# A two-layer hybrid backbone on one core: the passage between the layers and the norm behind the output projection, rearranged

## The reference, cut to what matters

```python
def rms_norm(x, g):
    return x * lax.rsqrt(jnp.mean(x * x, axis=-1, keepdims=True) + EPS) * g

def layer(x, ctx, ...):
    hx = modulate(rms_norm(x, g_pre_mix), sh1x, sc1x)       # first norm
    hc = modulate(rms_norm(ctx, g_pre_mix), sh1c, sc1c)
    px = hx @ w_in                                          # kv | q | conv b,c,u | fourier f | gates
    pc = hc @ w_in                                          # in the last layer only its kv columns
    ...                                                     # attention, short convolution, Fourier mixing
    x = x + g1x * rms_norm(yx, g_post_mix)                  # yx = (gated sum of branches) @ w_out
    hx2 = modulate(rms_norm(x, g_pre_ffn), sh2x, sc2x)      # second norm
    x = x + g2x * rms_norm(moe(hx2), g_post_ffn)            # the same for ctx in layer 0

def moe(t):
    scores = sigmoid(t @ w_router)                          # 32 experts, the best 4 of each token
    comb = weights of the four choices, scaled to sum 2.5
    routed = sum over choices of comb * expert(t)           # silu(t @ gate) * (t @ up) @ down
    return routed + shared_expert(t)
```

## Time and profile before

| what | value |
|---|---|
| median of three runs | 1566.01 us (1560.89, 1566.01, 1567.47) |
| the profiled execution: its own time | 1567.75 us |
| the profiled execution: span | 1566.0 us |
| PE busy | 1464.3 us (94%) |
| DVE busy | 947.9 us (61%) |
| ACT busy | 616.9 us (39%) |
| POOL busy | 326.2 us (21%) |
| mean granted TensorE clock | 0.979 of full |

### The profile page before, as it was taken

One profiled execution on the slowest core, in us unless ns is written; L12 is line 12 of the kernel. 1 busy time (PEld: TensorE's weight loads), 2 busy tenths in 40 slices (PEclk: granted clock), 3 DMA queues, 4 the chain that ended last, 5 costly groups with the idle time before them and its releaser, 6 DMA issues.

```text
span 1566.0 us, 22775 instructions
## 1 busy us (share of the span) xinstructions
PE 1464.3 (94%) x7739; PEld 1042.5 (67%) x7739; DVE 947.9 (61%) x1624; ACT 616.9 (39%) x1049; POOL 326.2 (21%) x392
## 2 busy tenths in 40 slices
PE   5999998899989899999999986999899899999996
PEld 2688575688867766777777744876799775555552
DVE  1777889779986466777777757446656641222222
ACT  2432235433324435656656524433555521111211
POOL 4000000001112003555556536000001021111200
PEclk9999999999999999999999997999999999999998
DMA  9943340266586155999999974516255459999993
GB/s 334 326 162 112 135 162 1 84 216 213 188 289 250 54 219 206 342 365 368 362 366 377 362 234 155 197 35 239 81 197 208 157 218 372 376 414 415 414 415 146
DMA packets 116888, 382.36 MB, mean 244 GB/s; under 512 B 13554, under 2 KB 18114, under 8 KB 98128
## 3 DMA queue, kind: packets, MB, share of 16 engines
q1 hardware_dynamic: 100976, 352.08, 59.6%
q0 software_dynamic: 14480, 26.11, 4.9%
q10 hardware_dynamic: 1360, 3.23, 0.5%
HBM read 382.05 MB, written 21.06 MB: 257 GB/s over the span
## 4 chain that ended last, share of the span: by engine, by line
PE 77%; DVE 9%; DMA 7%; ACT 2%; issue 2%; POOL 2%; SPq 0%; ACTq 0%; POOLq 0%; DVEq 0%
PE ps L1844 7%; PE ps L1814 6%; PE ps L1416 6%; PE ps L1643 4%; PE ps L1645 4%; PE ps L1644 4%; PE ps L1789 4%; PE ps L1788 4%; PE ps L1790 4%; PE ps L1847 4%; PE ps L1777 3%; DMA ring<-in_w_up_e 3%; PE ps L1539 2%; PE ps L1540 2%; PE ps L1541 2%; PE ps L1862 2%
## 5 line engine op out<-in xcount | busy, mean ns | idle before, releaser
L2464 DVE TENSOR_TENSOR ring_lo<-ring,m_lo 128x1024 fp32r<-128x1024 f32 x128 | 156.1, 1223 | 11.9 <-ACT m_lo L1285 2.4
L1285 ACT ACTIVATE m_lo<-ring 128x1024 fp32r<-128x1024 f32 x128 | 135.5, 1060 | 44.0 <-PE ps L1790 30.5
L1643 PE MATMUL ps<-ring_lo,w_hi 128*128 128x512 f32 (+1 forms) x384 | 131.4, 342 | 4.7 <-DVE ring_lo L2253 4.6
L2042 DVE SCALAR_TENSOR_TENSOR Grow<-ring,small,Grow 128x512 f32<-128x512 f32 x182 | 131.1, 749 | 3.8
L1644 PE MATMUL ps<-h_lo,w_hi 128*128 128x512 f32 (+1 forms) x384 | 130.3, 339 | 0.0
L1814 PE MATMUL ps<-ring,oT_b 128*64 128x256 f32 x1088 | 124.9, 382 | 1.5 <-DMA ring<-in_w_up_e 1.5
L2489 DVE COPY head<-ps 128x128 f32<-128x128 f32 (+1 forms) x67 | 23.8, 355 | 163.0 <-PE ps L1826 161.1
L917 POOL TENSOR_TENSOR qkv<-qkv,head 128x512 f32<-128x512 f32 (+1 forms) x32 | 37.0, 1157 | 384.4 <-DVE head L2299 384.4
L1814 PEld LDWEIGHTS ps<-ring,oT_b 128*64 128x64 f32 x1088 | 75.3, 137 | 42.2 <-issue 6.4
L1788 PE MATMUL ps<-m_lo,oT_lo 128*128 128x512 f32 x256 | 102.5, 401 | 0.0
L1790 PE MATMUL ps<-m_lo,h_lo 128*128 128x512 f32 x256 | 100.0, 391 | 0.0
(11 more groups left out here) (363 smaller groups left out, 3333.9 us busy)
## 6 DMA issues: line engine op xcount, KB each, us to landing
ring<-in_w_gate_e SPq DMA_DIRECT2D x67, 1024.0 KB, 7.9
ring<-in_w_up_e SPq DMA_DIRECT2D x66, 1024.0 KB, 6.9
ring<-in_w_ada SPq DMA_DIRECT2D x36, 1024.0 KB, 5.4
qkv<-in_w_down_e SPq DMA_DIRECT2D x34, 1024.0 KB, 10.6
ring<-in_w_in SPq DMA_DIRECT2D x13, 2048.0 KB, 11.1
cT<-in_w_down_e SPq DMA_DIRECT2D x16, 1024.0 KB
fT<-in_w_down_e SPq DMA_DIRECT2D x16, 1024.0 KB
qkv<-in_w_in SPq DMA_DIRECT2D x7, 2048.0 KB, 10.7
```

Source lines behind the costliest of these rows:

```text
L1285: nc.scalar.activation(pair(e_hi, j), pair(gu[u], j), ACT.Copy).then_inc(e_hi_ready, 1)
L1643: nc.tensor.matmul(dst[:, 0:n_tok], hi, h_hi_of[l][:, k, 0:n_tok], start=k == 0, stop=False)
L2042: ins = V.scalar_tensor_tensor(into, w[:, k, :], by, into, ALU.mult, ALU.add)
L2464: V.tensor_tensor(pair(gu_lo[u], j), pair(gu[u], j), pair(e_hi, j).bitcast(f32), ALU.subtract).then_inc(e_lo_ready, 1)
```

## The change

- **Image's last choice.** The load of choice 3 for the image is issued as two loads of 512 KB, one for each tile, with semaphores of their own. SP waits for the second to land before it issues the context's four loads.
- **Small vectors of layer 1.** They are issued by SP behind those loads and behind b's weights, no longer by GpSimd.
- **Context's choices 0 and 1** are added on TensorE: ScalarE writes four 128x128 diagonal matrices with the weights of tokens (`row_weight`, tiles 2 and 3, choices 0 and 1), and TensorE adds eight products of 512 columns to the shared expert's banks. They stand ahead of the image's transposition in its list.
- **Context's choices 2 and 3** are added on VectorE for both tiles, the first of them straight out of PSUM. GpSimd's part and ScalarE's `move_out` are gone.
- **Banks.** Layer 1's kv and q are put on other banks than the context's sums, so the image's transposition, kv and q no longer wait for `moved`; the context's transposition does.
- **Square root's table.** ScalarE takes a square root of one column ahead of the final roots, at the end of layer 0's and of layer 1's expert loop.
- **Second norm, both layers.** ScalarE's copy of the out products is gone. VectorE multiplies each half by the gate's row out of PSUM, each as soon as its square's sum is there, and the rest is one instruction (times the inverse root, plus `xres`). `normalise_x(t-1)` stands inside the loop. `transpose_late` opens all banks and transposes tiles 0 to `tiles`-3 in the two parts as before, then tile `tiles`-2 and the last one whole.

```diff
@@ plan()
-            first = [(by_half[j], "hx", j) for j in range(4)] + [("act", "kv", n) for n in range(2)] + [("act", "q", n) for n in range(act)]
+            for j in range(4):
+                g.add(by_half[j], l, "hx", j)
+            g.shift += 4
+            first = [("act", "kv", n) for n in range(2)] + [("act", "q", n) for n in range(act)]
...
-                g.add("act", l, "out", t, j)
+                g.add("dve", l, "out", t, j)
@@ SP, end of layer 0
-                    load_rows(3, 0)
+                    for t, landed in ((0, picked_loaded[3][0]), (1, second_loaded)):
+                        sp.dma_start(picked[3][0][:, t, :], y_rows.rearrange("(t p k) d -> p t k d", p=P, k=TOPK)[:, t, 3, :]).then_inc(landed, 16)
+                    sp.wait_ge(second_loaded, 16)
                     for r in range(TOPK):
                         load_rows(r, 1)
                     load_item(first_item[1] + 2)
+                    load_vectors(sp, 1)
@@ GpSimd, layer 1: the eight small loads and this are taken out
-                    for r in range(TOPK):
-                        row = picked[r][t // 2][:, t % 2, :]
-                        pool.wait_ge(picked_loaded[r][t // 2], 16)
-                        nc.gpsimd.tensor_scalar(row, row, pick_w[:, t, r:r + 1], None, ALU.mult).then_inc(added_by_pool, 1)
...
-                        nc.gpsimd.tensor_tensor(acc[:, t, :], acc[:, t, :], row, ALU.add).then_inc(added_by_pool, 1)
@@ ScalarE
                     for j in range(2):
                         wait_full(act_e, l, "out", t, j)
                         square(bank(l, "out", t, j), 12 + 2 * t + j, 512)
-                        nc.scalar.activation(rows[:, t % 2, 512 * j:512 * j + 512], bank(l, "out", t, j), ACT.Copy)\
-                            .then_inc(emptied["act"], 1)
...
                 if l == 0:
+                    nc.scalar.activation(row_weight[:, 0, 0, 0:1], ident[:, 0:1], ACT.Sqrt).then_inc(row_weight_ready, 1)
+                    act_e.wait_ge(row_weight_ready, 1)
+                    for t in range(2, NTILE):
+                        for r in range(ROWS_ON_PE):
+                            ins = nc.scalar.activation(row_weight[:, t - 2, r, :], ident[:, :], ACT.Copy, scale=pick_w[:, t, r:r + 1])
+                    ins.then_inc(row_weight_ready, 1)
                     add_square(0)
-                    move_out(2)
                     add_square(1)
-                    move_out(3)
...
                 else:
+                    nc.scalar.activation(late_junk[:, 0:1], ident[:, 0:1], ACT.Sqrt).then_inc(row_weight_ready, 1)
+                    act_e.wait_ge(row_weight_ready, 3)
                     add_square(0)
@@ TensorE
+                    for ks in (range(6), range(6, KC)):
+                        for k in ks:
+                            group(l, "h", n, k)
+                        for t in range(tiles - 2):
+                            transposed(t, ks)
+                    transposed(tiles - 2, range(KC))
+                    transposed(tiles - 1, range(KC))
...
                     transpose_half("hx", 0)
-                    pe.wait_ge(moved, 1)
                 kv(0)
                 kv(1)
...
-                    pe.wait_ge(moved, 2)
...
                 if l:
+                    pe.wait_ge(moved, 2)
                     transpose_half("hc", 2)
...
+                if l == 0:
+                    pe.wait_ge(row_weight_ready, 2)
+                for r in range(ROWS_ON_PE if l == 0 else 0):
+                    pe.wait_ge(picked_loaded[r][1], 16)
+                    for t in (2, 3):
+                        for hf in range(2):
+                            ins = nc.tensor.matmul(acc_of_tile(t)[:, 512 * hf:512 * hf + 512], row_weight[:, t - 2, r, :],
+                                                   picked[r][1][:, t - 2, 512 * hf:512 * hf + 512], start=False, stop=True, skip_group_check=True)
+                        if r == ROWS_ON_PE - 1:
+                            ins.then_inc(acc_full, 1)
@@ VectorE, layer 1's start
-                    dve.wait_ge(moved, 2)
-                    add_rows(3, range(TOPK), 0)
+                    for r in range(ROWS_ON_PE, TOPK):
+                        for t in (2, 3):
+                            row = picked[r][1][:, t - 2, :]
+                            dve.wait_ge(picked_loaded[r][1], 16)
+                            if r == ROWS_ON_PE:
+                                wait_acc(dve, 0, t)
+                                V.scalar_tensor_tensor(acc[:, t, :], row, pick_w[:, t, r:r + 1], acc_of_tile(t), ALU.mult, ALU.add).then_inc(moved, 1)
+                            else:
+                                dve.wait_ge(moved, t - 1)
+                                V.scalar_tensor_tensor(acc[:, t, :], row, pick_w[:, t, r:r + 1], acc[:, t, :], ALU.mult, ALU.add)\
+                                    .then_inc(combined, 1)
@@ VectorE, second norm
                     c = 12 + 2 * t
+                    dve.wait_ge(ssq_ready[l], counts["ssq"] + 1)
+                    V.tensor_tensor(rows[:, t % 2, 0:512], bank(l, "out", t, 0), gate_row(l, 0, t // 2)[:, 0:512], ALU.mult)\
+                        .then_inc(emptied["dve"], 1)
...
+                    V.tensor_tensor(rows[:, t % 2, 512:DM], bank(l, "out", t, 1), gate_row(l, 0, t // 2)[:, 512:DM], ALU.mult)\
+                        .then_inc(emptied["dve"], 1)
                     inverse_root(c, c + 1)
                     wait_emptied(dve, l, "out", t, 1)
-                    link(V.scalar_tensor_tensor(rows[:, t % 2, :], rows[:, t % 2, :], rstd[:, c:c + 1], gate_row(l, 0, t // 2),
-                                                ALU.mult, ALU.mult))
-                    V.tensor_tensor(xres[:, t, :], xres[:, t, :], rows[:, t % 2, :], ALU.add).then_inc(x_updated[l], 1)
+                    V.scalar_tensor_tensor(xres[:, t, :], rows[:, t % 2, :], rstd[:, c:c + 1], xres[:, t, :], ALU.mult, ALU.add)\
+                        .then_inc(x_updated[l], 1)
                     if t >= 1:
                         invert_norm(t - 1)
-                wait_full(dve, l, "out", act - 1, 1)
-                for t in range(act - 1):
-                    normalise_x(t)
+                        normalise_x(t - 1)
```

More of the change, by code:

```diff
@@ L402, in hybrid_layers @@
                   rows_in(flat_of(fT)) + rows_in(probsT_b[:, :]), rows_in(qkv[:, 4096:8192])]
-        ON_POOL = 2
+        ROWS_ON_PE = 2
+        row_weight = oT_b[:, 1024:2048].rearrange("p (i r c) -> p i r c", i=2, r=TOPK)
         scratch = lambda name, shape, dt: [nc.dram_tensor(f"{name}_{l}", shape(l), dt, kind="Internal").ap()
@@ L457, in hybrid_layers @@
         sdn_loaded = one("sdn_loaded")
-        acc_full, moved, added_by_pool = one("acc_full"), one("moved"), one("added_by_pool")
+        acc_full, moved, row_weight_ready = one("acc_full"), one("moved"), one("row_weight_ready")
         xt_full = by_layer("xt_full")
@@ L471, in hybrid_layers @@
         picked_loaded = [[one(f"picked_loaded_{r}_{i}") for i in range(2)] for r in range(TOPK)]
+        second_loaded = one("second_loaded")
         combined = one("combined")
@@ L679, in wait_acc, with load_vectors @@
             eng.wait_ge(acc_full, NTILE * l + t + 1)
+        def load_vectors(eng, l):
+            col = lambda a: a.rearrange("(k p) -> p k", p=P)
+            with nc.allow_non_contiguous_dma("one small vector a partition"):
+                vectors = [(gqk[:, 0:2], col(I["g_kv"][l])), (gqk[:, 2:5], col(I["g_q"][l])),
+                            (bgate, I["b_gate"][l].rearrange("(b k p) -> p b k", p=P, b=3)),
+                            (wr[:, :, :], I["w_router"][l].rearrange("(p k) e -> p k e", k=KC)),
+                            (brow, I["b_router"][l:l + 1, :].to_broadcast([P, NE]))]
+                vectors += [(convw[:, j, :], col(I["conv_w"][l][j])) for j in range(3)]
+                assert len(vectors) == VECTORS
+                for dst, src in vectors:
+                    eng.dma_start(dst, src).then_inc(params_loaded[l], 16)
         def wait_combined(eng, l, t):
-            if t == ON_POOL:
-                eng.wait_ge(added_by_pool, 2 * TOPK)
-            else:
-                eng.wait_ge(combined, 3 * l + min(t, 2) + 1)
+            eng.wait_ge(combined, t + 1)
         once_more = lambda l, u: 16 if u >= UNROLL - AHEAD[l] else 0
@@ L857, in _ @@
                     wait_arrived(pool, "ada", 3)
[L858 to L877 removed]
+                if l == 0:
+                    load_vectors(pool, l)
+                if l:
                     pool.wait_ge(x_updated[l - 1], 2 * ACTIVE[l - 1])
@@ L1361, in _ @@
                 take_y(3, last)
-                def move_out(t):
-                    wait_acc(act_e, 0, t)
-                    nc.scalar.activation(acc[:, t, :], acc_of_tile(t), ACT.Copy).then_inc(moved, 1)
                 def add_square(t, l=l):
@@ L1943, in _ @@
                     for hf in range(2):
```

(12 more changed lines are left out.)

40 lines of the change are left out of this document (9 added, 31 removed).

## The result

| | kernel before | changed kernel |
|---|---|---|
| median of four runs | 1565.28 us (1560.89 to 1567.47) | 1548.47 us (1543.85 to 1551.35) |
| ratio, 95% interval | | 0.9895 (0.9877 to 0.9912) |
| profiled execution: own time, span | 1567.75, 1566.0 us | 1551.35, 1549.4 us |

Of the profiled executions it is 16.4 us.

The account below looks back on a forecast made before the run. PE was taken as the bound, its work plus gaps: passage 9.0, second norms 3.3 and 0.5, tail 1.1, together 13.9 us off 1567.75, and 1.7 to the median: 1552.5 us forecast, range 1547 to 1559.

Parts of the forecast that it names:

- Image ready at 945.0: Passage: from VectorE's start on the last choice at 933.45, adding 1.3, 1.8 and 8.4 us, the image is normalised at 945.0.
- rival 1: Passage: eight products at the lower clock or rows late; passage gains 5 to 6 us, time 1556.5; rivals 1 or 2 alone 0.25.
- Products end at 949.2: PE ahead of the image's transposition: rows at 939.7, eight context products 6.95 us, clock restart 2.6; sets the start, 4.1 us earlier.
- b products at 973.1: End of the passage: DVE's path sets the b products at 973.1, before 981.31; gain 8.2 us, PE waiting 2.2 us.
- passage: PE from the shared expert to the b products and tiles: forecast gain 9.0 us, 8.2 plus 0.8 of clock.
- Second norm, layer 0: 3.3 us: Layer 0, out products to router's products: last tile's transposition 4.3 us earlier, less 1.0 for the clock.
- The 1.0 us charged for the clock in the router's products: Layer 0's second norm: clock may stay low into the router's products; bounds 0 and 2.5 us, 1.0 taken.
- Layer 1 0.5: Second norm of layer 1, two tiles: first transposition 0.8 us earlier, the last by half of it; gain 0.5 us.
- tail 1.1: Behind the last product: ACT's table load of 1.28 us leaves the path, less a handoff of 0.2; gain 1.1 us.
- rival 4: SP's queue: eight small loads hold SP so long that layer 1's c weights come late; slower, 1572 at 60 us; chance 0.03.
- The likeliest case: Whole kernel: the forecast and near it, a gain of 12 to 16 us; chance 0.45.
- rival 3: Everything better: full clock in the eight products (2.5 us) and in the router's (1.0); time 1549; chance 0.15.

Follow-up runs that it names:

- e10: Kernel before with one edit: layer 1's small vectors issued by SP behind the b weights, no longer by GpSimd; ratio 0.9986.
- e3: Changed kernel with layer 1's small vectors issued by GpSimd at their old place again; 1551.9 us, ratio 0.9926 to the kernel before.
- e9: Changed kernel with four products of a zero matrix filling TensorE's wait for the context's rows; ratio 0.9891 to the kernel before.
- e1: Kernel before with only the changed kernel's second norm, both layers; ratio 0.9967.
- e2: Changed kernel with the second norm put back as before, passage and early root kept; ratio 0.9930 to the kernel before.
- e4: Changed kernel with the four products of the context's choice 1 moved behind the image's transposition; ratio 0.9912 to the kernel before.
- e6: Changed kernel without SP's wait for the image's last choice ahead of the context's loads; 1546.9 us, ratio 0.9888 to the kernel before.
- e11: Changed kernel without SP's wait for the image's last choice, run again for more runs; ratio 0.9881 to the kernel before.
- e12: Changed kernel with a one-column copy in place of each early square root; one run only, tail 6.88 us against 5.80.

## Why the prediction was right

The prediction's times are those of the old trace. To compare them with the new one, they have to be moved by the 3.38 us by which the shared expert began earlier in it.

- **Image ready at 945.0, moved 941.6.** Measured 941.65, with the chain from the last choice at 11.54 us where 11.5 were forecast. The last choice was there when VectorE was; e10 and e3 show that the small vectors had been the cause. What rival 1 made of the rule of turns (the Trainium skill, DMA: Bandwidth & Descriptors, section Queues, rings and completion order), that such packets hardly hold up others, is not what e10 and the windows show. Its premise of packets of a few bytes is not borne out either: on GpSimd's queue all eight loads together were only 304 packets. So the rule itself is not tested here.
- **Products end at 949.2, moved 945.8.** Measured 945.57; they, not the image, set the start. The restart charged at 2.6 us was 1.5 to 2.8 (e9).
- **b products at 973.1, moved 969.7; b tiles 0.8 us shorter.** Measured 968.90 and 0.82. PE waits 1.06 us there, 2.2 were forecast: the context's chain was 0.8 us quicker than I had it, mostly in the four additions, which took 4.9 us and not 5.3. This is the passage's 9.85 against 9.0. Over all traces the passage's gain is 8.3 to 11.4: the old passage took 71.15 (e1) and 72.66 us, the new one 61.2 to 62.8.
- **Second norm, layer 0: 3.3 us.** The trace shows 4.4. The 1.0 us charged for the clock in the router's products did not come (3.74 us); the lower clock fell on the last tile's transpositions, 1.97 us. Against the old norm in e2 and e10 the gain is 3.3, the forecast's figure, but partly by luck: the earlier trace rows had made the old transpositions dear by 1.0 us, and the charge of 1.0 us that did not come cancels it.
- **Layer 1 0.5, tail 1.1.** Measured 0.6 and 1.0.
- **SP's small loads (rival 4).** They hold SP far longer than GpSimd, which was through all eight in 6.3 us before (925.03 to 931.37):

```profile
933.45 6.13 SPq L697 DMA_DIRECT2D small<-in_g_kv  x1
939.62 1.53 SPq L697 DMA_DIRECT2D small<-in_g_q  x1
941.19 1.88 SPq L697 DMA_DIRECT2D small<-in_b_gate  x1
943.11 6.30 SPq L697 DMA_DIRECT2D wr<-in_w_router  x1
```

Until 952.8, 19 us for all eight, where the rival needed 54; the c weights were issued at 967.87 and nobody waited for them.

Too small were the passage by 0.85 us and the norm by 1.1. What is left of the 16.4, 0.5 us, and the rest of the medians' 16.8 is scatter in stretches that were not touched. The likeliest case (a gain of 12 to 16 us) held for the four parts, 15.9, and just not for the whole.

The time itself, 1548.5, is rival 3's 1549 rather than the forecast's 1552.5, and not by rival 3's mechanism: the clock did fall ahead of the eight products, and of its two terms only the 1.0 us of the router's products came. The 4.0 us between forecast and result are 2.9 us of gain, 0.7 us by which the median of the kernel before was lower here (1565.28) than in the runs that the forecast started from (1566.01), and 0.3 to 0.4 us of rounding in the forecast (1567.75 - 13.9 - 1.7 is 1552.2).

What I did not see is that the gate (SP's wait for the image's last choice) had lost its reason. I computed that the rows would land at 939.7 because of it and that PE would fall to the lower clock, took both as given, and did not ask what the same transfers would do without it once the small vectors were gone.

## What to carry to other kernels

Price a change from the rows of its own stretch, stretch by stretch, and measure each stretch from a local mark (here the shared expert's start): differences of 2 us show so (two traces of the same kernel differed by 1.6), while the times of one kernel lie 3 to 10 us apart. When two cures for one delay go in together, try each without the other: moving the small loads had removed the cause, and the gate, meant for the same delay, cost 2 to 4 us of waiting and of clock in the traces. And an engine that is the bound gains little from work put in another order (e4), only from idle time taken out.

## What the runs showed of the hardware

- Loads written one element at a time cost more packets from SP's queue than from GpSimd's: q1 has 5,648 packets more than in the kernel before (100,976), and 5,632 more in e10, where nothing else was moved; q0 has only 304 fewer (14,480) in both. The first landed 15.4 us behind its issue behind large loads, against 3.6 us from GpSimd.
- While such loads ran from GpSimd's queue the DMA engines were 57 to 80% busy at 17 and 82 GB/s, and the load of 1 MB issued then took 8.1 us instead of 5.2.
- TensorE's clock fell in the wait of 3.38 us ahead of the context's rows and stayed at 1.2 GHz over more than 5 us of work behind it, until about 941.5; through waits of 1.52 and 1.58 us in e6 and e11 it stayed at 2.4 GHz (granted clock 1.00 from 928 to 946). The windows of the changed kernel (the column before the last two is the granted clock):

```profile
934.00:936.00 2.00, 0.17 (x1) 0.20 (x2) 1.80 (x3) 0.17 (x3) 0.00 (x0) 0.66 1.03 416
936.00:938.00 2.00, 2.00 (x3) 0.97 (x4) 1.83 (x3) 1.11 (x3) 0.00 (x0) 0.50 1.02 420
938.00:940.00 2.00, 2.00 (x3) 0.69 (x3) 1.70 (x4) 1.06 (x2) 0.00 (x0) 0.50 1.03 422
940.00:942.00 2.00, 2.00 (x4) 0.87 (x3) 1.20 (x4) 0.45 (x3) 0.00 (x0) 0.63 1.02 412
```

- The load of ScalarE's table cost 1.28 us on the path, with no drain beside it, in before and in e12.
